# Latent attention in split precision: weights and latents in high and low parts, plain and turned features in tiles of their own

## The reference

```python
    cq = _rmsnorm(b_cq, gq)              # 384 wide
    ckv = _rmsnorm(b_ckv, gkv)           # 256 wide
    qh = _split_heads(cq @ w_uq, MLA_HEADS)
    q_b = jnp.concatenate([qh[..., :MLA_NOPE], _rope(qh[..., MLA_NOPE:], pos)], axis=-1)
    kvh = _split_heads(ckv @ w_ukv, MLA_HEADS)
    k_rope = _rope(b_kr[:, None], pos)
    k_b = jnp.concatenate([kvh[..., :MLA_NOPE],
                           jnp.broadcast_to(k_rope, (B, MLA_HEADS, S, MLA_ROPE))], axis=-1)
    yb = mla_attention(q_b, k_b, kvh[..., MLA_NOPE:])
    yb = _merge_heads(yb) * jax.nn.silu(b_z)
```

## Time and profile before

| what | value |
|---|---|
| three runs | 2110.24, 2112.52 (median), 2115.38 us |
| span of the profiled execution | 2110.5 us (the page gives no other time for it) |
| mean granted TensorE clock | 0.997 |
| busy: PE, PEld, DVE, ACT, POOL | 2092.2, 1865.2, 1413.2, 1296.7, 654.3 us |

### The profile page before, as it was taken

How to read it: one execution, slowest core, us unless ns; L and a number is a source line. 1 busy time by engine, 2 the same in 40 slices (tenths; PEclk the granted TensorE clock), 3 DMA queues, 4 the chain that set the end, 5 groups by cost and what they waited for, 6 DMA issues and landing times.

```text
span 2110.5 us, 33552 instructions
## 1 busy us (share of the span) xinstructions
PE 2092.2 (99%) x13307; PEld 1865.2 (88%) x13311; DVE 1413.2 (67%) x1438; ACT 1296.7 (61%) x1436; POOL 654.3 (31%) x316
## 2 busy tenths in 40 slices
PE   9999999999999999999999999999999999999998
PEld 8979999988999999999998888888888888888887
DVE  1555223346322874233787999999999999999997
ACT  4556445456555534444536777777777777777776
POOL 5727886726787204987201000000000000000000
PEclk9999999999999999999999999999999999999999
DMA  7434555625555425655538999999999999999995
GB/s 246 139 112 151 178 197 157 184 83 160 160 192 170 137 84 180 201 187 172 171 110 286 385 370 342 374 356 371 352 357 360 365 368 341 370 356 371 369 364 200
DMA packets 307633, 529.06 MB, mean 251 GB/s; under 512 B 11842, under 2 KB 152802, under 8 KB 307520
## 3 DMA queue, kind: packets, MB, share of 16 engines
q1 hardware_dynamic: 306496, 525.92, 71.7%
q0 software_dynamic: 736, 1.00, 0.2%
q10 hardware_dynamic: 288, 0.52, 0.1%
HBM read 525.84 MB, written 1.05 MB: 250 GB/s over the span
## 4 chain that ended last, share of the span: by engine, by line
PE 92%; POOL 3%; DVE 3%; ACT 1%; DMA 1%; issue 1%; SPq 0%; DVEq 0%; POOLq 0%
PE bank L722 90%; POOL weights_low L3124 3%; PE bank L1555 1%; DVE qb L2384 1%; DMA ring<-in_w_ple_dram 0%; PE bank L956 0%; DMA ring<-in_w_in_dram 0%; ACT sc L1700 0%; PE bank L733 0%; DVE sc L2392 0%; ACT weights_high L1703 0%; ACT expert_weights_high L1703 0%; ACT xT L1700 0%; DVE y L2392 0%; DVE rot L2384 0%
## 5 line engine op out<-in xcount | busy, mean ns | idle before, releaser
L2384 DVE TENSOR_TENSOR expert_weights_low<-ring_experts,expert_weights_high 128x2048 fp32r<-128x2048 f32 x336 | 764.9, 2289 | 72.4 <-ACT expert_weights_high L1703 72.2
L1703 ACT ACTIVATE expert_weights_high<-ring_experts 128x2048 fp32r<-128x2048 f32 x336 | 646.6, 1925 | 166.9 <-PE bank L722 162.1
L3124 POOL TENSOR_TENSOR weights_low<-ring,weights_high 128x1024 fp32r<-128x1024 f32 x252 | 617.5, 2473 | 321.5 <-ACT weights_high L1703 211.1
L1703 ACT ACTIVATE weights_high<-ring 128x1024 fp32r<-128x1024 f32 x294 | 304.0, 1056 | 323.1 <-PE bank L722 290.4
L722 PE MATMUL bank<-x_high,weights_high 128*128 128x256 f32 x1024 | 229.2, 281 | 0.4 <-POOL weights_low L3124 0.2
L722 PE MATMUL bank<-x_high,weights_low 128*128 128x256 f32 x1024 | 225.6, 277 | 0.0
L722 PEld LDWEIGHTS bank<-x_high,weights_high 128*128 128x128 f32 x1024 | 183.6, 188 | 2.1 <-issue 0.8
L722 PEld LDWEIGHTS bank<-x_high,weights_low 128*128 128x128 f32 x1024 | 183.5, 188 | 0.5 <-issue 0.5
L722 PE MATMUL bank<-expert_weights_high,gathered_high 128*128 128x512 f32 x456 | 180.9, 397 | 0.3 <-DVE gathered_low L2392 0.3
L722 PE MATMUL bank<-expert_weights_high,gathered_low 128*128 128x512 f32 x456 | 178.0, 390 | 0.0
L722 PE MATMUL bank<-expert_weights_high,gathered_high_b 128*128 128x512 f32 x448 | 177.8, 397 | 0.0
(11 more groups left out here) (339 smaller groups left out, 3725.0 us busy)
## 6 DMA issues: line engine op xcount, KB each, us to landing
ring_experts<-in_moe_w_gate_dram SPq DMA_DIRECT2D x112, 1024.0 KB, 6.9
ring_experts<-in_moe_w_up_dram SPq DMA_DIRECT2D x112, 1024.0 KB, 6.7
ring_experts<-in_moe_w_down_dram SPq DMA_DIRECT2D x112, 1024.0 KB, 6.4
ring<-in_w_in_dram SPq DMA_DIRECT2D x62, 1024.0 KB, 5.3
ring<-in_w_merge_dram SPq DMA_DIRECT2D x24, 1024.0 KB, 5.1
ring<-in_w_out_dram SPq DMA_DIRECT2D x14, 1024.0 KB, 5.0
ring<-in_ffn_w_gate_dram SPq DMA_DIRECT2D x11, 1024.0 KB, 5.3
ring<-in_ffn_w_up_dram SPq DMA_DIRECT2D x11, 1024.0 KB, 5.4
```

The costliest lines, as they stand in the source:

```text
L1703: return nc.scalar.activation(dst, src, ACT.Copy, scale=scale)
L2384: return nc.vector.tensor_tensor(dst, x, z, op)
L3124: nc.gpsimd.tensor_tensor(half_of(wlo[:, q_slot, :], t, width), half_of(ring[:, slot, :], t, width), half_of(whi[:, q_slot, :], t, width). ...
```

## The change

- w_uq (two units of 384 columns instead of four of 192) and w_ukv (two of 512 instead of one of 1024) become a third kind of unit, "latent". ScalarE makes their high parts (`latent_high`), GpSimd the low parts, and that difference gives back the slot (`lat_lo`). The parts are laid out by kind of feature: plain features of all heads together, turned features together, keys and values apart.
- VectorE splits the scaled latents as well: scaled in place, copied to `cnh`, difference to `cnl`, first for the queries' latent, then for the other.
- The projections are un0, ur0, un1, ur1 (plain and turned features of the queries), kn0, kn1, mv0, mv1, of three matmuls each.
- Queries and keys have plain features in tiles of two heads (64 rows each) and turned features in tiles of four heads (32 rows each). A head's scores are the sum of two matmuls.
- The shared key is spread to four copies of 32 rows by one matmul (r4) before it is turned; one rk and one rq turn everything.
- The unit of 160 columns is two units of 128 and 32.

```diff
-    ("mc1", "a"), ("mc2", "a"), ("B", 2), ("ms", "a"), ("az0", "v"), ("V", 2), ("A", 3),
-    ("uq0", "a"), ("uq1", "a"), ("uq2", "a"), ("uq3", "a"),
-    ("rk", "v"), ("rq0", "v"), ("rq1", "v"), ("kn0", "a"), ("kn1", "a"), ("kn2", "a"),
-    ("kn3", "a"), ("rq2", "v"), ("rq3", "v"), ("mv0", "v"), ("mv1", "v"), ("B", 3),
+    ("mc1", "a"), ("mc2", "a"), ("B", 2), ("ms", "a"), ("r4", "a"), ("az0", "v"), ("V", 2), ("A", 3),
+    ("un0", "a"), ("ur0", "a"), ("un1", "a"), ("ur1", "a"), ("rk", "v"), ("kn0", "a"), ("mv0", "v"),
+    ("kn1", "a"), ("rq", "v"), ("mv1", "v"), ("B", 3),
...
-    + [("w_in", 2048, 256, 8), ("w_in", 2304, 256, 8), ("w_in", 2560, 160, 8), ("w_in", 1536, 256, 8)]
-    + [("w_uq", c, 192, 3) for c in range(0, 768, 192)] + [("w_ukv", 0, 1024, 2)]
+    + [("w_in", 2048, 256, 8), ("w_in", 2304, 256, 8), ("w_in", 2560, 128, 8), ("w_in", 2688, 32, 8), ("w_in", 1536, 256, 8)]
+    + [("w_uq", c, 384, 3) for c in (0, 384)] + [("w_ukv", c, 512, 2) for c in (0, 512)]
...
+            if kinds[v] == "latent":
+                return lat_lo.h, kinds[:v + 1].count("latent")
...
+                def latent_project(name, tiles, k, wh, wl, first):
+
+                    b = begin(name)
+                    for t in range(tiles):
+                        cols = slice(t * P, (t + 1) * P)
+                        for kk in range(k):
+                            mm(views(b)[:, t, :], wh[:, kk, cols], cnh[:, first + kk, :], kk == 0, False)
+                            mm(views(b)[:, t, :], wh[:, kk, cols], cnl[:, first + kk, :], False, False)
+                            ins = mm(views(b)[:, t, :], wl[:, kk, cols], cnh[:, first + kk, :], False, kk == k - 1)
                     ins.then_inc(full.h, 1)
...
+                    def qk_rope(m):
+
+                        r0 = HD * (m % 2) + ROPE * b
+                        part = slice(r0, r0 + ROPE)
+                        return qb[part, HEADS // 2 + m // 2, :], kr[part, :]
...
+                        ins = first(m, *qk(m), not split or m < 2)
+                    if split:
+                        for m in range(4):
+                            later(m, *qk_rope(m), False)
+                        for m in range(4):
+                            ins = first(m, *qk_rope(m), False)
...
+                    elif name == "r4":
+
+                        b = begin(name)
+                        mm(views(b)[:, 0, :], cst[0:ROPE, C_REP:C_REP + P], kr[0:ROPE, :], True, True).then_inc(full.h, 1)
...
+                def latent_high(i):
+
+                    n = layer * N_UNITS1 + LATENT_AT[layer][i]
+                    act.wait_ge(landed[n % RING].h, 16 * (n // RING + 1))
+                    for raw, (high, _) in latent_parts(layer, i):
+                        ins = copy(high, raw)
+                    ins.then_inc(lat_hi.h, 1)
...
-                copy(kr[HD:MLA_D, :], views(b)[HD:MLA_D, 1, :]).then_inc(dr_a.h, 1)
+                copy(kr[0:ROPE, :], views(b)[0:ROPE, 1, :]).then_inc(dr_a.h, 1)
+                latent_high(0)
+                latent_high(1)
                 take_turned(2)
                 b = G1.wait_full(act, layer, "ms")
                 inv_std(rstd[:, 0:2, :], views(b), 1, dr_a.h, drained_at(layer, "ms")).then_inc(std_done.h, 1)
+                b = G1.wait_full(act, layer, "r4")
+                copy(kr[:, :], views(b)[:, 0, :]).then_inc(dr_a.h, 1)
                 gate_tanh("az0", 0)
+                latent_high(2)
                 take_y(2)
+                latent_high(3)
                 exps(3)
-                for j in range(4):
-                    drain(layer, f"uq{j}", qb[0:MLA_D, 2 * j:2 * j + 2, :], MLA_D ** -0.5, slice(0, MLA_D))
-                for j in range(4):
-                    drain(layer, f"kn{j}", kb[0:HD, 2 * j:2 * j + 2, :], 1.0, slice(0, HD))
+                for j in range(2):
+                    drain(layer, f"un{j}", qb[:, 2 * j:2 * j + 2, :], MLA_D ** -0.5)
+                    b = G1.wait_full(act, layer, f"ur{j}")
+                    act.mul(qb[:, 4 + j, :], views(b)[:, 0, :], MLA_D ** -0.5).then_inc(dr_a.h, 1)
+                for j in range(2):
+                    drain(layer, f"kn{j}", kb[:, 2 * j:2 * j + 2, :])
...
-                act.wait_ge(kroped.h, kroped.at(layer, 1))
-                copy(kb[HD:MLA_D, :, :], kr[HD:MLA_D, :].unsqueeze(1).broadcast_to([ROPE, HEADS, S])).then_inc(
-                    kall.h, 1)
...
-                for t in range(5):
-                    ins = stt(cn[:, t, :], cq[:, t, :], par[:, P_GQ + t:P_GQ + t + 1], rstd[:, int(t >= 3), :],
-                              ALU.mult, ALU.mult)
-                ins.then_inc(ms_done.h, 1)
+                for part in (range(0, 3), range(3, 5)):
+                    for t in part:
+                        ins = stt(cq[:, t, :], cq[:, t, :], par[:, P_GQ + t:P_GQ + t + 1], rstd[:, int(t >= 3), :],
+                                  ALU.mult, ALU.mult)
+                    link(ins)
+                    part = slice(part[0], part[-1] + 1)
+                    link(nc.vector.tensor_copy(cnh[:, part, :], cq[:, part, :]))
+                    tt_(cnl[:, part, :], cq[:, part, :], cnh[:, part, :].bitcast(F32), ALU.subtract).then_inc(ms_done.h, 1)
...
-                for j in range(4):
-                    rope(f"rq{j}", qb[HD:MLA_D, 2 * j:2 * j + 2, :], j + 1).then_inc(rope_q.h, 1)
...
+                values(0)
+                rope("rq", qb[:, 4:6, :], 1).then_inc(roped.h, 1)
+                values(1)
...
+                    if q == SPLIT1.index("az0"):
+                        for i in range(LATENT1):
+                            pool.wait_ge(lat_hi.h, lat_hi.at(layer, i + 1))
+                            if i == 3:
+                                G1.wait_full(pool, layer, "ur0")
+                            for raw, (high, low_part) in latent_parts(layer, i):
+                                ins = nc.gpsimd.tensor_tensor(low_part, raw, high.bitcast(F32), ALU.subtract)
+                            ins.then_inc(lat_lo.h, 1)
```

More of the change, by code:

```diff
@@ L230 @@
 SPLIT_WEIGHTS = ("w_in", "w_merge", "w_a", "w_b", "w_c", "w_out", "w_pg")
-KINDS1 = [["split" if name in SPLIT_WEIGHTS and cols in (256, 512) else "plain" for name, _, cols, _ in units]
+KINDS1 = [["split" if name in SPLIT_WEIGHTS and cols in (256, 512) else "latent" if name in ("w_uq", "w_ukv") else "plain"
+           for name, _, cols, _ in units]
           for units in UNITS1]
 PLAIN1 = KINDS1[0].count("plain")
-assert N_UNITS1 - PLAIN1 == len(SPLIT1) and len(SPLIT1) % 2 == 0
+LATENT1 = KINDS1[0].count("latent")
+assert N_UNITS1 - PLAIN1 - LATENT1 == len(SPLIT1) and len(SPLIT1) % 2 == 0
+LATENT_AT = [[u for u, kind in enumerate(kinds) if kind == "latent"] for kinds in KINDS1]
 SPLIT_AT = [[u for u, kind in enumerate(kinds) if kind == "split"] for kinds in KINDS1]
@@ L926, in scores @@
                     else:
-                        pe.wait_ge(rope_q.h, rope_q.at(layer, 4))
-                        pe.wait_ge(kall.h, kall.at(layer, 1))
-                        G1.wait_drained(pe, layer, "kn3")
+                        pe.wait_ge(roped.h, roped.at(layer, 2))
+                        G1.wait_drained(pe, layer, "kn1")
                     if n >= 1:
                         pe.wait_ge(pT_ready.h, pT_ready.at(layer, n))
+                    split = kind == "mla"
                     def qk(m):
-                        if kind == "mla":
-                            return qb[0:MLA_D, 4 * b + m, :], kb[0:MLA_D, 4 * b + m, :]
@@ L940, in scores, with later, first @@
+                    def later(m, q, k, start):
+                        return mm(bank[4 + m % 2][:, (m // 2) * S:(m // 2) * S + S], q[:, P:S], k, start, not split,
+                                  share=split)
+                    def first(m, q, k, start):
+                        return mm(bank[6 + m % 2][:, (m // 2) * P:(m // 2) * P + P], q[:, 0:P], k[:, 0:P], start,
+                                  not split, share=split)
                     for m in range(4):
-                        q, k = qk(m)
@@ L1055, in step @@
                         b = begin(name)
-                        mm(bank[b][0:MLA_D, 0:width], cst[0:MLA_D, C_ROT:C_ROT + MLA_D], src,
-                           True, True).then_inc(full.h, 1)
+                        mm(bank[b][:, 0:width], cst[:, C_ROT:C_ROT + P], src, True, True).then_inc(full.h, 1)
                     elif name[:2] == "kn":
                         j = int(name[2])
+                        turn_to("latent")
                         if j == 0:
-                            kept[0] = take(1024, 2)
@@ L1062, in step @@
-                        w = kept[0]
+                            pe.wait_ge(ms_done.h, ms_done.at(layer, 2))
+                        pe.wait_ge(lat_lo.h, lat_lo.at(layer, 3 + j))
+                        latent_project(name, 2, 2, *(tiles_of(w, 2) for w in keys_w[j]), 3)
+                    elif name[:2] == "mv":
+                        wh, wl = (tiles_of(w, 2) for w in values_w[int(name[2])])
```

(12 more changed lines are left out.)

130 lines of the change are left out of this document (88 added, 42 removed).

## The result

| | before | changed |
|---|---|---|
| median of the runs | 2112.52 us | 2121.20 us |
| all runs | 2110.24 to 2115.38 | 2119.05 to 2121.51 |
| span of the profiled execution | 2110.5 us | 2117.9 us |
| mean granted TensorE clock | 0.997 | 0.993 |

The ratio is 1.004, with a 95% interval of 1.0028 to 1.0053: slower by some 8.7 us. No change was forecast; of the rivals, the one with the falling clock happened.

A forecast was written before the change was run, and what follows sets the result against it. TensorE, busy 99%, was taken as the bound; 11.5 us saved a layer, less waits and dearer scores, left 1.25 us, 2.5 in all: 2110.0 from the 2112.52 median, called no change, range 2100 to 2118.

The forecast's parts named there:

- the one with the falling clock: Rival, slower: TensorE's clock halves in the wait at rk; 2117 with one layer hit, 2123.6 with both; chance 0.22.
- Its chain: Layer 0, az0's load to az1: late loads and ScalarE's fixed order make TensorE wait; az1 starts 2.5 us earlier.
- az0's load: Moved one ring slot later, it lands 5.2 us later, at 103.9; TensorE's B step loses 0.4 us.
- V2's wait: After az0, TensorE waits 1.35 us for ScalarE's turned probabilities, which stand behind the second half of w_uq.
- the scores': Within the last diff scores (A3), TensorE idles 2.45 us waiting for take_y(2).
- az1's: Ahead of az1, TensorE idles 1.45 us for GpSimd's difference making az1's low part.
- The work: TensorE's latent projections, rk, rq and r4: 24.96 us removed, 13.5 put in; 10.7 us a layer saved after dearer scores.
- The next wait: At rk, behind un0's drain and the exponentials of diff batch 1: TensorE idle for 3.35 us.
- The 1.95: VectorE's time in us to finish the KV latents, ahead of az0's gate and the softmax of diff batch 1.
- GpSimd's new work: Four differences of about 1024 elements, 2.7 us each, put at nothing because they fit GpSimd's idle 41 us.
- the point at 3.8 us: Wait at rk from which the clock was said to fall, taken from the kernel's end; 3.35 was forecast there.
- The scores: Latent scores after V3, A4 and A5: 0.4 us dearer a batch, some 0.3 idle; together about 1.2 lost.

The follow-up runs named there:

- Experiment 5: Changed kernel with GpSimd's difference of w_ukv's first half waiting until VectorE has split the latents; 2110.86 us beside 2111.49 for the kernel before, ratio 0.9997.
- experiment 3: Changed kernel with TensorE's idle time filled by matmuls on zeros (3 ahead of V2, 8 within scores, 22 between ur0 and un1); 2115.65 us, ratio 1.0025 to before.
- experiment 2: Changed kernel with ScalarE's drains of un0, ur0, un1 and ur1 ahead of the exponentials of diff batch 1; 2123.68 us, ratio 1.0069 to before.
- experiment 4: Changed kernel with the 32-column unit's slot handed back by ms's first matmul instead of az0's; 2112.84 us, ratio 1.0012 to before.
- experiment 6: Changed kernel with matmuls on zeros only ahead of V2 (3) and within the last diff scores (8); 2118.70 us, ratio 1.0032 to before.

## Why the prediction was wrong

Its chain is in the trace step by step. Taking off the 0.85 us of the start: az0's load lands at 103.8 (forecast 103.9), B starts at 113.9 (114.1), the second half of w_uq is issued at 118.1 (118.3) and lands at 122.0 (122.3), take_y(2) ends at 129.2 (129.75), the diff scores at 129.9 (130.2). V2's wait was 0.85 (1.35), the scores' 1.87 (2.45), az1's 1.60 (1.45). The work was right too: 102 split matmuls, rk and rq as priced, r4 0.62 for 0.43.

The step that failed is in "The next wait": "VectorE finishes the KV latents (1.95) and az0's gate (0.6) at 131.5". The softmax behind them began at 133.45 instead. The 1.95 was summed from passes measured while GpSimd was idle (118.71 in the earlier trace rows); with GpSimd's difference beside them two of the passes took 3.00 us for 0.88. I had put GpSimd's new work at nothing because it fits GpSimd's idle time, and not asked whom it holds up. The price stood in the trace of the kernel before: beside GpSimd's differences from 147.04 on the earlier trace rows, a VectorE pass with two inputs in SBUF took 2.88 us; with GpSimd idle, the same pass took 0.67.

```profile
138.71 0.67 DVE L2384 TENSOR_TENSOR qb<-qb,cst 32x512 f32<-32x512 f32 x1
...
147.07 2.88 DVE L2384 TENSOR_TENSOR qb<-qb,cst 32x512 f32<-32x512 f32 x1
```

The 2.1 us went straight into the chain: exponentials at 137.5 for 135.7, rk at 141.8 for 139.75, a wait of 3.94 for 3.35. Experiment 5 takes away this one thing and comes close to the forecast: 0.6 us under before (the interval reaches from 2.5 under to 1.3 over), where 2.5 was summed, and az1 2.1 us earlier in layer 0, where 2.5 was summed.

The second step follows from it. The rival put the point at 3.8 us of waiting at rk and named those very passes as what would bring it there; rk to kn1 then ran largely at half the clock, 7.04 us up to rq instead of 4.55. So the rival had the right place and the right cause; what it cost was 2.3 to 3.0 us a layer (experiment 3) of the up to 6.8 that it priced, since the clock came back before mv1. Its point of 3.8 us does not hold as a rule: at rk the clock fell 2.1 us into the wait, and it had fallen at 130.5 after gaps of 0.85 and 1.87. That the measured wait, 3.94, lies just above it is luck. Of the three other waits, those at V2 and within the scores were about half a microsecond shorter than summed, the one at az1 as forecast.

The scores were mis-sized. Forecast: 0.4 us dearer a batch and 0.3 idle. Measured: 5.4 us from V3 to the end of A4 for 4.38, and in A5 3.8 for 2.7, so about 1.0 each. The 32-row matmuls took 1.5 us for the 1.4 summed; the 64-row ones, with the wait for take_y among them, 2.5 and 2.3 us for 1.6 and the 0.3 idle.

Put together for layer 0: 2.5 us forecast as won to az1, less 2.0 (rk later, GpSimd beside VectorE), 2.5 (rk to kn1, clock) and 0.4 (rq to az1), gives 2.4 lost; 2.51 is measured from V1 to V3. Layer 1 lost 3.82. With 2.1 for the scores of each layer that is 10.5 us, beside 8.75 up to the mixer (9.6 less the 0.85 of the start) and 8.7 in the medians; where 1.8 us come back ahead of the mixer is not shown.

## What to carry to other kernels

When an engine's idle time is to take new work, ask which engine it slows while it runs, as well as whether it fits; VectorE's passes with two SBUF inputs and GpSimd's differences must be laid apart in time. In an engine's fixed order, a step that waits for a late load belongs behind everything that another engine waits for: moving two lines on ScalarE turned 8.7 us lost into 6.5 to 8 won. A saving on the engine that is busy for 99% is only the sum's first line; each new wait has to be followed to the next one, and waits close together can cost the clock as well. What a new neighbour costs may already stand in the trace: look for a place where the two engines work side by side today.

## What the hardware showed that was not expected

The clock fell from 2.4 to 1.2 GHz after two idle gaps of 0.85 and 1.87 us with small matmuls between (changed kernel, layer 0), and with gaps of 0.82 and 1.86 it held (experiment 5, layer 0). It fell in each of the eight waits of 3.80 us or more (changed kernel and experiments 2, 4 and 6, both layers), 2.0 to 4.7 us after TensorE had stopped; in one of 3.16 us after dense matmuls it held (experiment 5).

Two VectorE passes over 384 elements took 5.21 us instead of 1.15 beside GpSimd's differences (experiment 2), while a pass that reads PSUM took 0.41 as ever.
